# Two transformer stacks on one core: square roots on ScalarE, post-norm scaling on VectorE, modulation sums behind the weight splits, and two of the first four modulation blocks multiplied by TensorE

## The reference

```python
h = modulate(x, norm_g[l, 0], sh1, sc1)                       # rms_norm(x, g) * (1 + scale) + shift
x = x + 0.5 * g1[:, None] * swiglu(h, ff_w13[l, 0], ff_w2[l, 0])
h = modulate(x, norm_g[l, 1], sh2, sc2)
x = x + g2[:, None] * mixer(h)                                # hybrid conv + MLA, or NSA attention
h = modulate(x, norm_g[l, 2], sh3, sc3)
x = x + 0.5 * g3[:, None] * swiglu(h, ff_w13[l, 1], ff_w2[l, 1])
```

## Time and profile before

| what | value |
|---|---|
| runs | 2525.79, 2526.31, 2539.52 us; median 2526.31 |
| profiled execution | 2526.72 us, span 2524.9 us |
| granted TensorE clock, mean | 0.932 |
| PE busy | 2252.9 us, 89% of the span |
| DVE busy | 1547.4 us, 61% |
| ACT busy | 946.2 us, 37% |
| HBM read | 415 MB, mean 165 GB/s |

### The profile page before, as it was taken

One profiled execution on the slowest core, in us unless ns is written; L12 is line 12 of the kernel. 1 busy time (PEld: TensorE's weight loads), 2 busy tenths in 40 slices (PEclk: granted clock), 3 DMA queues, 4 the chain that ended last, 5 costly groups with the idle time before them and its releaser, 6 DMA issues.

```text
span 2524.9 us, 41719 instructions
## 1 busy us (share of the span) xinstructions
PE 2252.9 (89%) x17470; PEld 2207.7 (87%) x17470; DVE 1547.4 (61%) x2128; ACT 946.2 (37%) x1209; POOL 113.2 (4%) x68
## 2 busy tenths in 40 slices
PE   2999868898899988989999997978998998987998
PEld 2999868898899988979998997868998998977998
DVE  7666675666766653656447555976556555575654
ACT  2333423333333344433334334224334333434433
POOL 0000000000000000000000001630000000000000
PEclk9999889899999987989998998988998998998999
DMA  6466533466556533114544552213453553411552
GB/s 275 196 256 257 207 139 134 175 250 257 203 227 261 226 137 132 50 51 184 183 167 152 183 182 100 101 40 143 173 192 120 200 183 133 159 59 67 200 182 83
DMA packets 52942, 417.58 MB, mean 165 GB/s; under 512 B 5873, under 2 KB 6001, under 8 KB 6769
## 3 DMA queue, kind: packets, MB, share of 16 engines
q1 hardware_dynamic: 52848, 416.27, 43.9%
HBM read 415.20 MB, written 1.05 MB: 165 GB/s over the span
## 4 chain that ended last, share of the span: by engine, by line
PE 59%; DVE 20%; DMA 10%; ACT 5%; issue 4%; POOL 1%; SPq 1%; DVEq 0%; ACTq 0%
PE AB L259 10%; PE AB L261 10%; PE AB L260 10%; DMA raw<-slabs 10%; DVE ada_acc L1357 7%; PE Y L259 6%; PE Y L260 6%; PE Y L261 6%; DVE lo L1328 4%; ACT hi L954 4%; DVE qT L1903 2%; PE M L524 2%; PE Y L721 2%; PE Y L736 1%; PE M L752 1%
## 5 line engine op out<-in xcount | busy, mean ns | idle before, releaser
L1328 DVE TENSOR_TENSOR lo<-raw,hi 128x2048 fp32r<-128x2048 f32 x322 | 748.5, 2326 | 632.5 <-ACT hi L954 632.3
L259 PE MATMUL AB<-h_hi,hi 128*128 128x256 f32 x3072 | 880.7, 287 | 12.6 <-DVE ada_raw L1913 5.8
L260 PE MATMUL AB<-h_lo,hi 128*128 128x256 f32 x3072 | 875.1, 285 | 0.0
L261 PE MATMUL AB<-h_hi,lo 128*128 128x256 f32 x3072 | 874.8, 285 | 0.0
L954 ACT ACTIVATE hi<-raw 128x2048 fp32r<-128x2048 f32 x322 | 614.6, 1910 | 645.3 <-DMA raw<-slabs 249.2
L259 PEld LDWEIGHTS AB<-h_hi,hi 128*128 128x128 f32 x3072 | 595.8, 194 | 15.3 <-DVE ada_raw L1913 6.8
L260 PEld LDWEIGHTS AB<-h_lo,hi 128*128 128x128 f32 x3072 | 595.9, 194 | 0.1
L261 PEld LDWEIGHTS AB<-h_hi,lo 128*128 128x128 f32 x3072 | 595.4, 194 | 0.0
L259 PE MATMUL Y<-g_hi,hi 128*128 128x256 f32 x1280 | 372.8, 291 | 53.0 <-DVE g_lo L1535 53.0
L261 PE MATMUL Y<-g_hi,lo 128*128 128x256 f32 x1280 | 370.4, 289 | 0.0
L260 PE MATMUL Y<-g_lo,hi 128*128 128x256 f32 x1280 | 370.3, 289 | 0.0
(11 more groups left out here) (291 smaller groups left out, 2274.7 us busy)
## 6 DMA issues: line engine op xcount, KB each, us to landing
raw<-slabs SPq DMA_DIRECT2D x322, 1024.0 KB, 4.8
ada_raw<-ada SPq DMA_DIRECT2D x35, 2048.0 KB, 7.8
x<-x_t SPq DMA_DIRECT2D x1, 1024.0 KB, 10.1
kT<-ada SPq DMA_DIRECT2D x1, 1024.0 KB, 18.4
vt<-ada SPq DMA_DIRECT2D x1, 1024.0 KB, 20.4
out_t<-x SPq DMA_DIRECT2D x4, 256.0 KB, 2.4
vec<-vectors SPq DMA_DIRECT2D x1, 462.0 KB, 3.5
hf<-constants SPq DMA_DIRECT2D x1, 401.0 KB, 15.1
```

The costliest lines, as they stand in the source:

```text
L259: nc.tensor.matmul(out_, w_hi, r_hi, start=start, stop=False, **kw)
L260: nc.tensor.matmul(out_, w_hi, r_lo, start=False, stop=False, **kw)
L261: return nc.tensor.matmul(out_, w_lo, r_hi, start=False, stop=stop, **kw)
L1328: nc.vector.tensor_tensor(lo[slot][:, :], raw[slot][:, :], hi[slot][:, :].bitcast(F32), ALU.subtract).then_inc(lo_done[slot], 1)
```

## The change

Four things are changed.

1. **The FFN step on DVE.** mac comes last in the body, behind the splits of w_(i-1) and a_(i+1) and gate_lo. The first body, i = 1, is written out ahead of the loop and has the same order.
2. **The reciprocal root** of most norms (norm 0 to 5, 7 and 10, the six adds of the second stack, and final): ACT takes Sqrt of the mean square (`deviation`), DVE its reciprocal and one Newton step (`root_of_sqrt`). POOL's fourth addition goes; PE sums five pieces instead of four. A Sqrt of one column is put at the end of each block (`sqrt_table`), so that ACT's table is in place; the FFNs of the second stack and the inner norms of the mixers keep the old root.
3. **Adds of the second stack:** the scaling of Y by the gain goes from ACT to DVE, behind the squares.
4. **begin:** blocks 1 and 3 are multiplied by TensorE straight from the loaded weights (32 one-column products each, `matvec`), blocks 0 and 2 stay with DVE; loads are in the order of use; twice ten 512-column products of zeros (`keep_warm`) run ahead; the first two slabs are split before norm 0 instead of one.

```diff
@@ DVE, the step of an FFN
                     if not first:
                         split(sb_, i + nb)
+                    split(sw, i + nw)
+                    gate_lo(i + (g0 - 1))
                     if out_:
                         mod_out(i + (q0 - 2))
+                    if a:
+                        split(sa, i + (na + 1))
                     if mac_:
                         mac(0, i + (q0 - 1), i + (a0 - 1))
-                    split(sw, i + nw)
-                    gate_lo(i + (g0 - 1))
-                    if a:
-                        split(sa, i + (na + 1))
@@ SP, the loads of the loop (two blocks fewer are counted, the wait is for the same sum)
-                        load_ada(0, i + q0, i * KD + KD * q0)
+                        load_ada(0, i + q0, i * KD + KD * (q0 - ADA_PE))
@@ SP, begin and the start of FFN 0
                 sp.dma_start(vec[:, :], vec_in).then_inc(vec_loaded, 16)
                 load_ada(0, 0, None)
-                sp.dma_start(x[:, :, :], x_in).then_inc(x_loaded, 16)
-                load_ada(1, 1, None)
-...
                 for n, to in enumerate((kT[:, :, :].rearrange("p k t -> p (k t)"),
                                         vt[:, :, :].rearrange("p a b -> p (a b)"))):
-                    sp.dma_start(to, ada_in[2, :, n * SLAB:(n + 1) * SLAB]).then_inc(ada_in_[2], 16)
+                    sp.dma_start(to, ada_in[1, :, n * SLAB:(n + 1) * SLAB]).then_inc(ada_in_[2], 16)
+                sp.dma_start(x[:, :, :], x_in).then_inc(x_loaded, 16)
+                sp.dma_start(hf[:, :, :].rearrange("p k t -> p (k t)")[:, 0:NCON], con_in).then_inc(con_loaded, 16)
+                load_ada(1, 2, None)
+                sp.dma_start(qT[:, 0, :].bitcast(I32), pos_in.partition_broadcast(P)).then_inc(pos_loaded, 16)
                 load_ada(0, 3, KD)
+                next_slab()
+                next_slab()
...
+                if f == 0:
+                    sp.wait_ge(ada_first, ADA_BEGIN)
+                    load_ada(0, q0, None)
@@ PE, begin
                 pe.wait_ge(const_ready, 1)
-                cols(0)
-                stat_tree(hf)
-                for q in range(1, 4):
-                    cols(q)
+                pe.wait_ge(act_ready, 1)
+                pe.wait_ge(ada_in_[0], 16)
+                keep_warm(10)
+                pe.wait_ge(ada_in_[2], 32)
+                matvec(1, 2)
+                acc_cols(0, 1, ada_acc)
+                tree_sums(hf)
+                keep_warm(10)
+                acc_cols(2, 2, gf)
+                pe.wait_ge(ada_in_[0], 32)
+                matvec(3, 0, between=spread)
@@ PE, the sums of a norm
-                s0, p0 = c.take("sq", KD), c.take("pair", 4)
-                sums([(pair_ready, p0 + 3, sq[:, 0, :]), (pair_ready, p0 + 4, sq[:, 4, :]),
-                      (sq_ready, s0 + 7, sq[:, 6, :]), (sq_ready, s0 + 8, sq[:, 7, :])], ones[1024])
+                s0, p0 = c.take("sq", KD), c.take("pair", 3)
+                sums([(sq_ready, s0 + 5, sq[:, 4, :]), (sq_ready, s0 + 6, sq[:, 5, :]),
+                      (pair_ready, p0 + 3, sq[:, 0, :]), (sq_ready, s0 + 7, sq[:, 6, :]),
+                      (sq_ready, s0 + 8, sq[:, 7, :])], ones[1024])
@@ ACT
+            def deviation():
+
+                act.wait_ge(stat_ready, c.take("stat") + 1)
+                nc.scalar.activation(root[:, :], M[:, 0:TT], ACT.Sqrt, bias=eps_[:, 0:1]).then_inc(sqrt_ready, 1)
+
+            def sqrt_table():
+
+                nc.scalar.activation(eps_[:, 1:2], eps_[:, 0:1], ACT.Sqrt)
@@ DVE, the root
+            def root_of_sqrt():
+
+                c.take("stat")
+                vh, tmp = var[:, 0:TT], var[:, TT:2 * TT]
+                dve.wait_ge(sqrt_ready, c.take("sqrt") + 1)
+                nc.vector.tensor_scalar(vh, M[:, 0:TT], EPS, -0.5, ALU.add, ALU.mult).then_inc(dve_link, 1)
+                c.take("link")
+                link(nc.vector.reciprocal(root[:, :], root[:, :]))
+                for t in range(TT):
...
@@ DVE, an add of the second stack
-                rstd_of(EPS, copy=False)
                 yg0 = (n - 6) * KD
+                for k in range(KD):
+                    if k % 2 == 0:
+                        dve.wait_ge(sq_ready, SQ_DONE["add", n] - KD + k + 2)
+                    nc.vector.tensor_scalar(hf[:, k, :], Y[:, k, :], gate[:, k:k + 1],
+                                            gate_bias[:, k:k + 1] if n == 7 else None, ALU.mult,
+                                            *([ALU.add] if n == 7 else [])).then_inc(yg_ready, 1)
+                root_of_sqrt()
+                dve.wait_ge(rstd_ready, c["stat"])
```

More of the change, by code:

```diff
@@ L289, in program, with ada_chunks, first_bank @@
                 n_sq += 3
-            if kind == "norm":
-                SQ_DONE[a[0]] = n_sq
+            if kind == "norm" or kind == "add" and a[0] >= 6:
+                SQ_DONE[kind, a[0]] = n_sq
         ADA_FFN = {0: (4, 10), 1: (16, 10), 2: (26, 8), 3: (34, 2)}
         ADA_MIX = (14, 15)
+        ADA_BEGIN = 4
+        ADA_PE = 2
+        def ada_chunks(buf):
+            if buf < 2:
+                w = ada_raw[:, buf, :].rearrange("p (k n) -> p k n", k=KD)
+                return [w[:, k, :] for k in range(KD)]
+            return [t[:, 2 * k:2 * k + 2, :].rearrange("p a b -> p (a b)") for t in
+                    (kT[:, :, :], vt[:, :, :].rearrange("p a (b t) -> p (a b) t", t=T)) for k in range(KD // 2)]
+        def first_bank(q):
+            return [y_bank(2), AB[:, 0, :], AB[:, 1, :], y_bank(3)][q]
         LEAD = {"mla": 1, "nsa": 2, "diff": 2}
@@ L510, in cols, with keep_warm, acc_cols, matvec @@
                 mm.then_inc(ada_cols, 1)
+            def keep_warm(n):
+                for _ in range(n):
+                    nc.tensor.matmul(N[:, :], zero_b[:, 0:P], zero_b[:, :], start=True, stop=True)
             def begin():
-                pe.wait_ge(const_ready, 1)
-                cols(0)
-                stat_tree(hf)
-                for q in range(1, 4):
-                    cols(q)
+                def acc_cols(q, n, acc):
+                    pe.wait_ge(ada_mac, n * KD)
+                    for j in range(PAIR):
+                        mm = nc.tensor.matmul(first_bank(q)[:, j:j + 1], acc[:, j * P:(j + 1) * P], one[:, 0:1],
+                                              start=True, stop=True)
+                    mm.then_inc(ada_first, 1)
+                def matvec(q, buf, between=None):
+                    w = ada_chunks(buf)
+                    for j in range(PAIR):
+                        if j == PAIR - 1 and between:
+                            between()
+                        for k in range(KD):
+                            mm = nc.tensor.matmul(first_bank(q)[:, j:j + 1], w[k][:, j * P:(j + 1) * P],
+                                                  cact[:, k:k + 1], start=(k == 0), stop=(k == KD - 1))
+                    mm.then_inc(ada_first, 1)
+                pe.wait_ge(const_ready, 1)
+                pe.wait_ge(act_ready, 1)
[9 more added lines that the diff above has]
+                matvec(3, 0, between=spread)
             def sums(parts, ones_):
@@ L1194, in hybrid @@
                 turn(4, first=4)
+                c.take("stat", 2)
+                sqrt_table()
                 next_slab()
@@ L1374, in begin @@
                 dve.wait_ge(act_ready, 1)
-                mac(0, 0, 0)
-                mod_out(0)
+                mac(0, ADA_PE, 0)
                 dve.wait_ge(con_loaded, 16)
@@ L1389, in begin @@
                                       ).then_inc(const_ready, 1)
-                mac(1, 1, 0)
-                rstd_of(EPS, copy=False)
-                mod_out(1)
-                mac(2, 2, 1)
-                mod_out(2)
-                mac(0, 3, 1)
-                ahead(1)
-                mod_out(3)
+                mac(1, ADA_PE + 1, 0, gf)
+                root_of_sqrt()
+                first_mod(1, 1)
+                first_mod(0, 2)
+                ahead(2)
+                first_mod(2, 3)
+                first_mod(3, 4)
+                dve.wait_ge(rstd_ready, c["stat"])
                 c["ada0"] = 2
@@ L1457, in root_of @@
                                                 ).then_inc(root_ready, 1)
+            def root_of_sqrt():
+                c.take("stat")
+                vh, tmp = var[:, 0:TT], var[:, TT:2 * TT]
[4 more added lines that the diff above has]
+                for t in range(TT):
+                    y = root[:, t:t + 1]
+                    nc.vector.scalar_tensor_tensor(tmp[:, t:t + 1], y, y, vh[:, t:t + 1], ALU.mult, ALU.mult
+                                                   ).then_inc(dve_link, 1)
+                at = c.take("link", TT)
+                for t in range(TT):
+                    y = root[:, t:t + 1]
+                    dve.wait_ge(dve_link, at + t + 1)
+                    nc.vector.scalar_tensor_tensor(y, tmp[:, t:t + 1], 1.5, y, ALU.add, ALU.mult
```

(1 more changed line is left out.)

87 lines of the change are left out of this document (46 added, 41 removed).

## The result

The changed kernel takes 2642.11 us (median; 2637.47 to 2645.48), the kernel before on the same chip 2526.05 (2525.35 to 2539.52). The ratio is 1.0445, with a 95% interval from 1.0406 to 1.0484: **slower by 4.5%, some 116 us**. The forecast was 2620, with a range from 2588 to 2655. The profiled executions give 2637.47 against 2526.7; their spans stand 110.6 us apart, where the sum of the steps said 94.

The account below looks back on a forecast made before the run. The prediction took the FFN loop through DVE, SP and DMA as the bound, not PE. Its terms, 131 - 13 - 27 + 3 = +94 on the profiled 2526.7, gave 2620.7, so 2620 us, range 2588 to 2655.

Parts of the forecast that it names:

- The bound: FFNs 0 to 3: a loop through sum, block load, slab load, copy and split sets the 20.6 us period, not PE.
- Part 1, the sum last: FFNs 0 to 3: the sum last in DVE's step lengthens the period by 5.4 us to 26.0, together +131 us.
- the end corrections: FFN ends: PE finishes 6 us (FFN 0, 1) or 8 us (FFN 2, 3) sooner; no last split of a, 2.2.
- Part 2, begin: begin: norm 0 starts between 39 and 53 us; gain 0 to 15, taken as -13 us.
- some 3 back: begin: the rotary angles, no longer hidden behind late slabs, take some 3 us of the gain back.
- Part 3, adds and roots: Second stack's adds -19 us, norms' roots and sums 9 less a little; -27 in all, between -12 and -35.
- Part 4, table loads: ACT: 19 more table loads, two of them ahead of the first sum in FFNs 0 and 2; +3 us, bound 24.
- That loads don't land in order: FFN steps: b, w and a share bandwidth, b lands with a; period 30.6, 120 us more, 2740; chance 0.06.
- That the load doesn't wait for the sum: FFN steps: b is under way before the sum ends, so PE sets the period; total about 2432; chance 0.06.
- That PE stays at the lower level: FFN steps: PE falls to the lower clock, becoming the bound at 36.5 us; up to +275 on the forecast; chance 0.04.
- Cancelling gains: Whole kernel: splits of a and w partly hidden, other gains at their ends; within 25 us of before; chance 0.03.

Follow-up runs that it names:

- e1: The changed kernel with the sum put back ahead of the splits of w and a and of gate_lo on DVE: 2502.13 us.
- e2: The kernel before with only DVE's FFN step order changed, the sum last: 2658.26 us.
- e3: The changed kernel with each modulation block's load issued one step later, behind b, w and a of the step that uses it: 2423.88 us.
- e5: e3 without the twenty products of zeros in begin: 2422.7 us.
- e6: e3 with ACT's rotary tables built behind the first body of FFN 0 instead of ahead of it: 2416.79 us.
- e7: e3 with block 3 summed by DVE again, so that TensorE multiplies only block 1: 2416.45 us.
- e8: e3 with ACT scaling Y by the gain again in the second stack's adds, the new root kept: 2432.68 us.
- e10b: e3 without the Sqrt instructions that load ACT's table ahead of time, so it loads with the root itself: 2419.92 us.
- e4: The changed kernel with the sum early as in e1 and the block's load behind slab b, ahead of w and a: 2431.21 us.
- e9b: e3 with the edits of e6 and e7 together: 2414.5 us.

## Why the prediction was right, point by point

**The bound.** Read as the loop through sum, block load, slab load, copy, split: confirmed. e1, e2 and e3 turn it on and off with one edit each, and the period follows: 20.7, 26.0, 18.2 us.

**Part 1, the sum last.** Forecast a period of 26.0 and +131 us for the FFNs, +134 with the two table loads; measured 26.1 to 26.2 and +136.7. The row-by-row schedule held: the first split began 12.5 us behind the end of the sum before (124.70, and 138.3 less a period; forecast 12.4), no gap over 0.25 us followed up to the sum. FFN 3's share, +0.6 for a forecast 3, and FFN 0 and 1 with 3.6 each above 46 show that the end corrections (-6, -2.2, -8) were rough; they were the weakest working of this part, and their errors partly cancelled.

**Part 2, begin. This step failed.** Forecast -13, measured -3.5, and that though the bounds 0 to -15 held it. Norm 0 starts at 49.17, not near 40, the same as 49.12 before. Three things were wrong.

- *The products of TensorE.* 7.6 us at the full level were taken; block 1 took 11.2 (14.44 to 25.6) and block 3 12.1 (35.87 to 48.9, less the spread between). All of a block at the slow pace is 13.7 (e5, eight rows 1.71 apart), not the forecast's 15, so both lie between the two figures. "cols ran at the full level among long matmuls" was no ground for a long run of one-column products.
- *What opens block 3.* The forecast had DVE's second sum (29.6) and one cols ahead of it, hence 30.6. DVE's sum was done at 28.95, but PE was not: block 1's products and a cols took it to 27.3, norm 0's own sums, which the forecast left out, took 4.41, then came the zero products and another cols. Block 3 started at 35.87.
- *The zero products.* "cost nothing, since PE waits for loads beside them" is right at 9.57 and wrong at 31.97, where nothing was waited for; 3.1 us went, of which 2.5 came back as faster products (e5).

The late start makes up 5.3 of the 10.4 us by which block 3 ended late (48.9 for 38.5), the products and the spread between them 5.1. What was gained, -3.5, is a slab copy that starts at 68.12 instead of 71.59. by_chunk itself gained 7.9 us: its last product starts at 64.12, before at 71.99 (the forecast had its end near 57). Then PE waits 2.25 us for the split of b_1, whose copy stood behind the rotary angles; the forecast had "some 3 back" for them, and e6 shows 3.1. e7 shows what the idea gives with one block on TensorE only: the gain at 42.36.

**Part 3, adds and roots.** Forecast -27, measured -26. In the add n = 8, from the start of PE's last down to its spread were 13.6 us; forecast about 10, measured 10.1, from 2037.88 to 2048.00. These rows of the changed kernel (PE, then DVE) show both ends, and the eight scalings that are done before the root begins:

```profile
2037.88 0.36 PE L261 MATMUL Y<-z_hi,hi 128*128 128x256 f32 x1 [0.52 <-DVE z_lo L1623]
...
2048.00 1.12 PE L582 MATMUL N<-ident,root 128*128 128x128 f32 x4 [1.20 <-DVE root L1543]
```

```profile
2043.83 3.23 DVE L1705 TENSOR_SCALAR hf<-Y,gate 128x256 f32<-128x256 f32 x8
2047.13 0.16 DVE L1532 TENSOR_SCALAR var<-M 128x2 f32<-128x2 f32 x1
```

For the adds alone, with their roots, the forecast was 19: five times 3.6, and 1. From PE's last product to its spread the six became shorter by 2.5, 4.2, 3.5, 2.2, 3.2 and 0.6 us, 16 together. e8, which takes back the scaling but keeps the roots, is 13.1 us longer from the first add to the last. So the adds were a little over-sized, 16 for 19, and the roots and sums of the norms bring the other 10, for a forecast of 9 less a little: small errors on two sides that nearly cancel.

**Part 4, table loads.** +3 was taken, with 24 as the bound. The two new loads ahead of a silu, in FFN 0 and FFN 2, are there (70.04 and 789.40 in the changed kernel, 1.3 us each), but no run takes them away, so the +3 is argued, not shown. e10b moves the 13 loads of the Sqrt table from begin and the ends of the blocks to right ahead of the root, and its time didn't rise. The Trainium skill ("ScalarE: Activation LUTs", What ACT_TABLE_LOAD costs) sets a drain on top of each load; e10b's Sqrt runs 0.34 us behind the load's end, behind a wait of 0.33 for PE, and where nothing is waited for the next instruction starts 1.29 us after the load does, as in the earlier trace rows. No trace here shows a drain.

**What the sum left out.** The NSA stage took 3.5 us more: 216.1 instead of 212.2 from its variance to its gate with its work unchanged, at a granted clock of 0.83 instead of 0.85, less 0.4 in its norm. With begin's 9.5, the loops' 2.7 and part 3's 1 it makes the 17 us by which 94 fell short.

**The rivals.** That loads don't land in order: b, w and a were issued within 2 us, and ACT starts the copies of b and w at 122.76 and 125.30, 2.54 us apart, just as the earlier trace rows had them; that rival would have had b land with a. That the load doesn't wait for the sum: it does, in nine waits. Its price was well worked out all the same: 2432 for a kernel in which b needn't wait, and e3 and e4, which make it so, take 2424 and 2431. That PE stays at the lower level: from 100 to 250 us its granted clock was 0.88, and it still waited for DVE. PE's idle time was 5.1 to 6.7 us a step behind the first, for a forecast of some 7. Cancelling gains: no.

## What to carry to other kernels

Where an engine's queue issues loads in order, a load that waits for a consumer holds up all loads behind it; write down the round trip (consumer's end, issue, landing, copy, split, consumer) and count everything that the consumer's engine does in between as paid in full. Then move the waiting load behind the loads that the next step needs first, before moving work on the computing engine: here reordering the work cost 5.4 us a step, and moving the load took 7.9 off again. An engine that is busy 88 or 89% of the span may still be far from its own bound in the stages that count: a chain of waits and the issue times of one queue showed it, the shares didn't.

## What the runs showed of the hardware that had not been expected

**Long runs of one-column fp32 products ran at little more than half pace on a busy TensorE.** Four of them took 1.84 us with PE busy in 34.2 of the 36 us from 14 to 50, and 1.03 just behind 4.4 us of 512-column products, for three chunks; in e3, with the same products ahead, 1.86 from the first. Why the products of zeros lift them in one kernel and not in another stays open. Norm 0 starts at 49.17, 55.21, 51.31, 49.07 and 48.73 in five kernels whose begin is alike or nearly so (the changed kernel, e3, e6, e8, e10b). The granted clock in the windows doesn't follow it: for 14 to 32 us it is 0.59 in the changed kernel and 1.00 in e3, where the products were slow throughout.

```profile
14.00:32.00 18.00, 17.32 (x93) 17.29 (x95) 9.45 (x24) 2.79 (x9) 2.14 (x3) 0.59 0.97 389
```

```profile
14.00:32.00 18.00, 17.54 (x82) 17.18 (x81) 9.77 (x25) 2.56 (x8) 2.13 (x3) 1.00 0.94 391
```

(The first is the changed kernel, the second e3; the number ahead of the last two is the granted clock.) Here the duration of the products themselves is the safer reading.

**One stage, the same work, 111 to 120 us.** The hybrid stage, from the last root of norm 1 to its gate, has nearly the same work in all kernels and took 111.2 us (granted clock 0.86, e3), 111.3 (0.87, e5), 112.9 (0.84, e8), 114.1 (0.84, the changed kernel), and 118.2 to 119.6 (0.78 to 0.80) in e6 and e7, 118.3 in e9b and e10b. Against e3, it cost e7 8.4 of its 16 us. e10b changes only where the Sqrt table is loaded and e6 only when the rotary tables are built, so the move of block 3 isn't the cause, or not the only one. What decides it stays open: no run here changed that stage alone.
